# Opening of a two-block network on one core: the first sixteen weight tiles by halves, with GpSimd making half of their low parts

## The chip, the cores and the metric

One core of one Trainium2 chip runs the whole program in one launch. The metric is the device time in microseconds (us) of one execution; the value shown for a kernel is the median of several runs. Engines are named as in the profile: TensorE is PE (its weight loads PEld), VectorE is DVE, ScalarE is ACT, GpSimd is POOL, and the queue that issues most loads is that of SyncE (SP).

## What is computed

Two blocks of layers follow each other on 256 tokens of width 1024, all in float32. The opening of the first is what matters here: a normalised and modulated input is multiplied by an input projection.

```python
def hybrid_layer(x, c, cos, sin, pre_g, post_g, w_ada, b_ada, w_in, w_out):
    B, S, _ = x.shape
    mod = jnp.einsum('bd,de->be', jax.nn.silu(c), w_ada) + b_ada
    shift, scale, gate = jnp.split(mod, 3, axis=-1)
    h = rms_norm(x, pre_g) * (1 + scale[:, None, :]) + shift[:, None, :]
    proj = jnp.einsum('bsd,de->bse', h, w_in)
    qa, ka, va, ga, qb, kb, vb, gb = jnp.split(proj, SPLIT_POINTS, axis=-1)
...
    y = jnp.einsum('bse,ed->bsd', jnp.concatenate([o_a, o_b], axis=-1), w_out)
    y = rms_norm(y, post_g)
    return x + gate[:, None, :] * y
```

`w_ada` is 1024 x 3072 and `w_in` 1024 x 4096. Two such layers (with attention in the part left out) are followed by feed-forward layers, a mixer and a spatial gating unit, which the change does not touch.

## The kernel before

**Products.** A weight tile is 256 rows by 512 columns, held as 128 partitions x 2 x 512 (512 KB); the whole program streams 428 of them. A float32 product is made of three products of rounded parts: ScalarE copies the tile into a buffer `sb_hi` as its high part (type fp32r), VectorE subtracts that from the tile and leaves the low part in the tile's own place (`sb_w..r`). The rows are turned so that the 1024 inputs lie on partitions, in eight chunks of 128 inputs x 256 tokens; they too have a high and a low part (`sb_hT`). TensorE multiplies high by high ("h"), low rows by high weights ("a") and high rows by low weights ("l"), for two groups of 128 tokens and two chunks: twelve matmuls of 128x512 a tile.

**Modulation.** `shift` and `scale` of the first layer come from sixteen tiles of `w_ada` (512 KB each, `sb_w<-in_mw`), two for each chunk of rows. VectorE multiplies such a tile by the condition vector and sums along it in one custom instruction (`dve_vector`, `CUSTOM_DVE_ANT_0 sb_w<-sb_w,sb_rows`), and adds the bias and multiplies the gain in two tiny instructions (`dve_first_end`). The rows of a chunk can be made only after that.

**Order of the opening.** Nothing is scheduled at run time: each engine runs its instructions in the order in which the program writes them (`pe_block1`, `act_block1`, `dve_block1`, `pool_start`, `sp_program`), with waits on semaphores. Before, the first four tiles (two chunks of rows for q, k, v and another q) go through `pe_first_tiles`, which multiplies the first two tiles chunk by chunk, and tiles 4 to 15 go through `pe_unit` one whole tile at a time. TensorE turns all the rows first (`pe_norm`, sixteen transposes). `act_block1` copies the turned rows out of PSUM (`raw`), makes the rows of two chunks at a time (`act_turned`, `act_high`) and the high part of one whole tile at a time (`act_tick`). `dve_block1` mixes whole low parts (`dve_tick`), modulation vectors (`dve_vector`) and the rows' low parts (`dve_low`). GpSimd makes a reciprocal root and fourteen tiny instructions for the angles of the rotary tables (`pool_rope_tables`), then loads the attention mask `blk`. SyncE's queue (`stream_order`) sends two modulation tiles and the first weight tile, two more modulation tiles, three weight tiles, four modulation tiles, and then weight and modulation tiles in turn. `place_stream` gives every load a slot from `release_time`; a load into a slot that is in use waits for its release, and everything behind it in the queue waits with it.

**Behind the opening.** Tiles 16 and up follow, with the attention of the first heads in between: the transposes of q and k (`tq`, `tk`), and the first scores (`("A", 0)`) after tile 15.

## Time and profile before

| | |
|---|---|
| median of 3 runs | 1588.73 us (1588.63 to 1588.76) |
| the profiled execution's own time, first to last instruction (span) | 1587.4 us |
| TensorE busy | 1565.0 us, 99% |
| VectorE busy | 1173.0 us, 74% |
| ScalarE busy | 777.5 us, 49% |
| GpSimd busy | 70.5 us, 4% |
| DMA over the span | 336.97 MB, 212 GB/s on average |

The profile is of one execution. No time is given for it but its span, which is 1.3 us under the median of the runs; sums are made against the span and carried over to the median. A busy TensorE is not TensorE at its peak, since its matmuls overlap. In the timeline a row is one or several like instructions in a run, with start, duration, engine, line, operation, tiles and count, and in square brackets the idle time of the engine just before it and what ended it. Durations of instructions that follow each other overlap a little: a 128x1024 subtraction of VectorE is listed with 1.22 us, and the next starts 1.14 us behind its start.

### The profile page before, as it was taken

The numbers are of one execution on the slowest core, as the hardware profiler recorded it, in microseconds if no ns is written. First come the engines' busy times: TensorE is split into PE (matmuls) and PEld (weight loads), VectorE is DVE, ScalarE is ACT, GpSimd is POOL, SyncE is SP. The second block draws the span as 40 slices with busy tenths as digits, with TensorE's granted clock in tenths as the row PEclk, the third lists the DMA queues.
The fourth block names the chain that finished last, engine by engine and source line by source line (L and its number), as shares of the span: only waits on it lengthen the run. The fifth ranks groups of instructions, "written<-read, shape, count | busy, mean of one in ns | idle before, by whom it ended". The sixth has DMA issues, their size and how long they took to land.

```text
span 1587.4 us, 20744 instructions
## 1 busy us (share of the span) xinstructions
PE 1565.0 (99%) x7994; PEld 1296.9 (82%) x7994; DVE 1173.0 (74%) x1917; ACT 777.5 (49%) x1246; POOL 70.5 (4%) x112
## 2 busy tenths in 40 slices
PE   7999999999999999999999999999999999999998
PEld 5887778888888888887777888888888888888887
DVE  7889899759886665477766888868877667666654
ACT  5767666532222222254556555445555463455552
POOL 2000000100000000030010100000000100010000
PEclk9999999999999999999999999999999999999999
DMA  9977676336656655252122777867777575455550
GB/s 376 373 290 273 234 251 224 107 127 231 213 212 239 224 212 179 87 175 80 67 95 72 281 302 292 311 219 264 255 280 274 210 308 187 171 203 187 186 190 30
DMA packets 93044, 336.97 MB, mean 212 GB/s; under 512 B 10625, under 2 KB 11265, under 8 KB 92690
## 3 DMA queue, kind: packets, MB, share of 16 engines
q1 hardware_dynamic: 90706, 327.58, 57.0%
q0 software_dynamic: 2240, 8.06, 1.5%
q8 instruction: 63, 1.03, 0.3%
q14 instruction: 35, 0.29, 0.1%
HBM read 334.56 MB, written 1.05 MB: 211 GB/s over the span
## 4 chain that ended last, share of the span: by engine, by line
PE 55%; DVE 2%; ACT 1%; issue 0%; POOL 0%; POOLq 0%; DVEq 0%; ACTq 0%
PE bank L292 53%; PE bank L295 2%; DVE sb_tm L301 0%; ACT sb_XN L298 0%; DVE sb_X L301 0%; ACT sb_arena L298 0%; ACT sb_XC L298 0%; DVE sb_arena L319 0%; DVE sb_arena L312 0%; DVE sb_XN L301 0%; DVE sb_sg L316 0%; DVE sb_XC L301 0%; DVE sb_w7r L301 0%; POOL sb_rstd L301 0%; DVE sb_w5r L301 0%
## 5 line engine op out<-in xcount | busy, mean ns | idle before, releaser
L292 PE MATMUL bank<-sb_hT,sb_hi 128*128 128x512 f32 (+1 forms) x1856 | 574.7, 379 | 0.0
L298 ACT ACTIVATE sb_hi<-sb_w 128x1024 fp32r<-128x1024 f32 x428 | 431.1, 1052 | 281.3 <-DMA sb_w<-in_w 238.1
L292 PEld LDWEIGHTS bank<-sb_hT,sb_hi 128*128 128x128 f32 x1856 | 332.1, 188 | 58.5 <-issue 0.2
L292 PE MATMUL bank<-sb_hi,sb_hT 128*128 128x512 f32 x1152 | 369.7, 395 | 2.9 <-ACT sb_hT L298 1.3
L292 PEld LDWEIGHTS bank<-sb_hi,sb_hT 128*128 128x128 f32 x1152 | 215.6, 188 | 53.2 <-issue 5.3
L312 DVE CUSTOM_DVE_ANT_0 sb_w<-sb_w,sb_cb 128x1024 f32<-128x1024 f32 x144 | 175.0, 1220 | 0.0
L301 DVE TENSOR_TENSOR sb_sg<-bank,sb_sg 128x512 f32<-128x512 f32 (+1 forms) x90 | 58.9, 660 | 101.5 <-ACT sb_sg L298 79.7
L298 ACT ACTIVATE sb_sg<-bank 128x512 f32<-128x512 f32 (+1 forms) x98 | 54.8, 573 | 118.0 <-PE bank L292 117.7
L298 ACT ACTIVATE sb_arena<-bank 128x512 f32<-128x512 f32 (+1 forms) x106 | 56.3, 558 | 55.9 <-PE bank L292 32.4
L301 DVE TENSOR_TENSOR sb_tm<-bank,sb_rows 128x512 f32<-128x512 f32 (+1 forms) x41 | 28.1, 684 | 69.5 <-PE bank L292 66.6
L298 ACT ACTIVATE sb_XN<-sb_X 128x512 f32<-128x512 f32 x33 | 20.7, 629 | 99.4 <-DVE sb_X L301 91.5
L301 POOL TENSOR_TENSOR sb_rstd<-sb_rstd,sb_minus_half 128x1 f32<-128x1 f32 (+1 forms) x23 | 14.1, 614 | 1159.0 <-DVE sb_rstd L309 1159.0
L301 DVE TENSOR_TENSOR sb_w1r<-sb_w,sb_hi 128x1024 fp32r<-128x1024 f32 x42 | 51.1, 1217 | 15.4 <-ACT sb_hi L298 15.3
L312 DVE CUSTOM_DVE_ANT_0 sb_w<-sb_w,sb_rows 128x1024 f32<-128x1024 f32 x48 | 57.9, 1221 | 0.8 <-DMA sb_w<-in_mw 0.8
L301 DVE TENSOR_TENSOR sb_w3r<-sb_w,sb_hi 128x1024 fp32r<-128x1024 f32 x42 | 51.4, 1224 | 9.4 <-ACT sb_hi L298 9.3
L301 DVE TENSOR_TENSOR sb_w2r<-sb_w,sb_hi 128x1024 fp32r<-128x1024 f32 x41 | 49.9, 1218 | 7.5 <-ACT sb_hi L298 7.3
L301 DVE TENSOR_TENSOR sb_w0r<-sb_w,sb_hi 128x1024 fp32r<-128x1024 f32 x40 | 48.7, 1218 | 9.0 <-ACT sb_hi L298 9.0
L301 DVE TENSOR_TENSOR sb_w5r<-sb_w,sb_hi 128x1024 fp32r<-128x1024 f32 x36 | 43.9, 1220 | 10.7 <-ACT sb_hi L298 10.7
L312 DVE CUSTOM_DVE_ANT_0 sb_tmw<-sb_w,sb_cb 128x1024 f32<-128x1024 f32 x40 | 48.8, 1220 | 0.9 <-DVE sb_XN L301 0.5
L292 PE MATMUL bank<-sb_hT,sb_w0r 128*128 128x256 f32 (+1 forms) x152 | 47.7, 326 | 0.0
L301 DVE TENSOR_TENSOR sb_w4r<-sb_w,sb_hi 128x1024 fp32r<-128x1024 f32 x32 | 39.0, 1217 | 9.5 <-ACT sb_hi L298 9.5
L301 DVE TENSOR_TENSOR sb_w6r<-sb_w,sb_hi 128x1024 fp32r<-128x1024 f32 x34 | 42.0, 1234 | 5.1 <-ACT sb_hi L298 5.1
(483 smaller groups left out, 3211.4 us busy)
## 6 DMA issues: line engine op xcount, KB each, us to landing
sb_w<-in_w SPq DMA_DIRECT2D x428, 512.0 KB, 4.3
sb_w<-in_mw SPq DMA_DIRECT2D x192, 512.0 KB, 4.8
sb_rows<-in_na_rpb POOLq DMA_DIRECT2D x16, 96.0 KB, 2.9
sb_X<-in_x SPq DMA_DIRECT2D x1, 1024.0 KB, 4.9
sb_cb<-in_cvec POOLq DMA_DIRECT2D x2, 512.0 KB, 8.8
sb_XC<-in_ctx POOLq DMA_DIRECT2D x1, 1024.0 KB, 12.8
sb_arena<-in_sg_ln_g POOLq DMA_DIRECT2D x1, 1024.0 KB, 7.2
sb_arena<-in_sg_ln_b POOLq DMA_DIRECT2D x1, 1024.0 KB, 10.5
```

The source lines that it names most:

```text
L292: return self.e.matmul(out, a, b, start=start, stop=stop)
L295: return self.e.transpose(out, a, ident)
L298: return self.e.activation(out, a, f, **kw)
L301: return self.e.tensor_tensor(out, a, b, op)
L312: return self.e.tensor_tensor_reduce(out=out, in0=a, in1=b, scale=scale, scalar=init, op0=op0, op1=op1, accum_out=accum)
```

## The change

The first sixteen weight tiles are cut into halves, one for each chunk of 128 rows. The work goes in eight steps, one for each chunk of the rows: steps 0 to 5 have four half tiles, step 6 three and step 7 five (`FIRST_UNITS`, `FIRST_STEPS`). SyncE's queue sends a step's two modulation tiles and then its half tiles. In each step VectorE makes the low parts of tiles 0 and 1 of the four and the two modulation vectors for the next step; GpSimd makes the low rows and the low parts of tiles 2 and 3. ScalarE makes the high rows straight from the turned rows, the half tiles' high parts, and the rows' values for GpSimd's subtraction. TensorE takes a step's four halves with all "h" terms first, then "a", then "l". The mask's load stays behind these instructions in GpSimd's program, and the instructions for the angles are spread between them.

```diff
+FIRST_UNITS = [(4 * c2 + i, k) for c2 in range(3) for k in range(2) for i in range(4)]
+FIRST_UNITS += [(12, 0), (13, 0), (14, 0), (12, 1), (13, 1), (15, 0), (14, 1), (15, 1)]
+FIRST_STEPS = [FIRST_UNITS[4 * i:4 * i + 4] for i in range(6)] + [FIRST_UNITS[24:27], FIRST_UNITS[27:]]
...
-    out = [("m", 0), ("m", 1), ("w", 0), ("m", 2), ("m", 3), ("w", 1), ("w", 2), ("w", 3)]
-    out += [("m", n) for n in range(4, 8)]
-    for n in range(4, 16):
-        out += [("w", n)] + [("m", n + 4)] * (n < 12)
+    out = []
+    for step in range(8):
+        out += [("m", 2 * step), ("m", 2 * step + 1)]
+        out += [("w", n, k) for n, k in FIRST_STEPS[step]]
...
+        def act_half_high(e, n, k):
+
+            e.wait_ge(*half_landed(n, k))
+            if HPREV[n] >= 0:
+                e.wait_ge(*done(USED, HPREV[n]))
+            e.act(HI_[HB[n]][:, k, :], ring[SLOT["w", n]][:, k, :], ACT.Copy).then_inc(
+                HI.sem, HI.put(n, *(() if k else (0,))))
...
+        def pool_half_low(e, n, k):
+            s = SLOT["w", n]
+            e.wait_ge(*high_ready(n, k))
+            e.tt(ring_r[s][:, k, :], ring[s][:, k, :], HI_[HB[n]][:, k, :].bitcast(F32), ALU.subtract).then_inc(
+                PO.sem, PO.put("low", n, k))
...
+        def act_first_high(e, ch):
+            t, h, _ = first_rows(ch)
+            e.wait_ge(*modulated("a0sc", ch))
+            e.wait_ge(*done(AE, "raw", ch // 2))
+            e.act(h, t, ACT.Identity, scale=mods[:, TG["a0sc"], ch:ch + 1], bias=mods[:, TG["a0sh"], ch:ch + 1]).then_inc(
+                AE.sem, AE.put("hh", "a0", ch))
...
+        def pool_first_low(e, ch):
+            t, h, l = first_rows(ch)
+            e.wait_ge(*done(AE, "t", "a0", ch))
+            e.tt(l, t, h.bitcast(F32), ALU.subtract).then_inc(PO.sem, PO.put("hl", "a0", ch))
...
+            for step in range(1, 6):
+                for term in "hal":
+                    for i in range(4):
+                        pe_first(e, step // 2 * 4 + i, step % 2, term)
+            for n, k in FIRST_UNITS[24:]:
+                pe_first(e, n, k, "hal")
+                if k or n == 15:
+                    items({(12, 1): 12, (15, 0): 13, (14, 1): 14, (15, 1): 15}.get((n, k)))
...
+                for step in range(1, 8):
+                    units = [u for u in FIRST_STEPS[step] if u != (0, 1)]
+                    if step == 6:
+                        act_rope_tables(e)
+                    act_first_high(e, step)
+                    act_half_high(e, *units[0])
+                    act_first_value(e, step)
+                    for n, k in units[1:]:
+                        act_half_high(e, n, k)
...
+                for step in range(8):
+                    for n, k in FIRST_STEPS[step]:
+                        if n % 4 < 2:
+                            dve_half_low(e, n, k)
+                    if step < 7:
+                        dve_vector(e, 2 * step + 2)
+                        dve_vector(e, 2 * step + 3)
...
+            for step in range(8):
+                if step:
+                    pool_first_low(e, step)
+                for n, k in FIRST_STEPS[step]:
+                    if n % 4 >= 2:
+                        pool_half_low(e, n, k)
+                for _ in range(3):
+                    next(rope, None)
```

How instructions move, first on VectorE, in the middle of the opening. Before, two whole low parts and two vectors stand there (`sb_w..r` is a low part, `sb_w` with `sb_rows` a vector, the line with 128x2 the end of a chunk pair's modulation):

```order
L301 TENSOR_TENSOR sb_w0r<-sb_w_49,sb_hi_78 128x1024
L312 ISA sb_w_51,sb_mods<-sb_w_51,sb_rows_81 128x1024
L312 ISA sb_mods 128x1
L301 TENSOR_TENSOR sb_mods<-sb_mods,sb_vec 128x2x2
L301 TENSOR_TENSOR sb_mods<-sb_mods,sb_vec 128x2
L301 TENSOR_TENSOR sb_w3r<-sb_w_55,sb_hi_71 128x1024
L312 ISA sb_w_57,sb_mods<-sb_w_57,sb_rows_81 128x1024
L312 ISA sb_mods 128x1
L301 TENSOR_TENSOR sb_hT<-sb_sg_84,sb_hT 128x512
```

Now, at a like place (step 3 of the change), each low part is half as long, the pair of them stands together, and the two vectors follow:

```order
L309 TENSOR_TENSOR sb_w10r<-sb_w_118,sb_hi_75 128x512
L309 TENSOR_TENSOR sb_w11r<-sb_w_120,sb_hi_76 128x512
L320 ISA sb_w_130,sb_mods<-sb_w_130,sb_rows_81 128x1024
L320 ISA sb_mods 128x1
L320 ISA sb_w_132,sb_mods<-sb_w_132,sb_rows_81 128x1024
L320 ISA sb_mods 128x1
L309 TENSOR_TENSOR sb_mods<-sb_mods,sb_vec 128x2
L309 TENSOR_TENSOR sb_mods<-sb_mods,sb_vec 128x1
```

Behind this place VectorE has two half low parts for every two vectors, where it had two whole ones and the rows' low part; the second half low part stands ahead of both vectors.

GpSimd, whose program before has only these tiny instructions between the reciprocal root and the mask's load (its end is shown):

```order
L301 TENSOR_TENSOR sb_ang<-sb_kk_100,sb_ang 128x32
L305 TENSOR_SCALAR sb_kk_100<-sb_kk 128x32
L301 TENSOR_TENSOR sb_ang<-sb_kk_100,sb_ang 128x32
L305 TENSOR_SCALAR sb_ang<-sb_ang 128x16
L306 TENSOR_SCALAR sb_ang<-sb_ang 128x32
L331 DMA sb_arena<-in_blk 128x768
```

Now, in steps 4 and 5 (`sb_hT` is the low rows of a chunk):

```order
L309 TENSOR_TENSOR sb_hT<-sb_sg_84,sb_hT 128x256
L309 TENSOR_TENSOR sb_w6r<-sb_w_61,sb_hi_73 128x512
L309 TENSOR_TENSOR sb_w7r<-sb_w_63,sb_hi_74 128x512
L309 TENSOR_TENSOR sb_hT<-sb_sg_84,sb_hT 128x256
L309 TENSOR_TENSOR sb_w6r<-sb_w_61,sb_hi_73 128x512
L309 TENSOR_TENSOR sb_w7r<-sb_w_63,sb_hi_74 128x512
```

Three subtractions a step have come in, the rows' first, and they stand ahead of the mask's load.

ScalarE in step 4 of the change, with high rows, half tiles and the rows' value in one order:

```order
L306 ACTIVATE sb_hT<-sb_sg_84,sb_mods 128x256
L306 ACTIVATE sb_hi_71<-sb_w_49 128x512
L306 ACTIVATE sb_sg_84<-sb_sg_84,sb_mods 128x256
L306 ACTIVATE sb_hi_72<-sb_w_51 128x512
L306 ACTIVATE sb_hi_73<-sb_w_61 128x512
L306 ACTIVATE sb_hi_74<-sb_w_63 128x512
L306 ACTIVATE sb_hT<-sb_sg_84,sb_mods 128x256
```

The high rows of the next chunk are the last of these rows; they stand behind the fourth half tile, and the next step's half tiles stand behind them.

## Rows read from the trace of the kernel before

**Rows 1.** The page, busy time and share of each engine.
```profile
PE 1565.0 (99%) x7994; PEld 1296.9 (82%) x7994; DVE 1173.0 (74%) x1917; ACT 777.5 (49%) x1246; POOL 70.5 (4%) x112
```

**Rows 2.** Timeline of PE in the opening: start and duration in us, count, idle before.
```profile
9.39 3.94 PE L295 MATMUL bank<-sb_cst,sb_XN 128*128 128x128 f32 x16 [3.27 <-ACT sb_XN L298]
...
13.02 1.23 PE L292 MATMUL bank<-sb_hi,sb_hT 128*128 128x512 f32 x4
...
16.13 1.20 PE L292 MATMUL bank<-sb_hi,sb_hT 128*128 128x512 f32 x4 [1.22 <-ACT sb_hi L298]
...
21.48 1.07 PE L292 MATMUL bank<-sb_hi,sb_hT 128*128 128x512 f32 x4
...
24.20 1.07 PE L292 MATMUL bank<-sb_hi,sb_hT 128*128 128x512 f32 x4
...
28.41 0.47 PE L292 MATMUL bank<-sb_hi,sb_hT 128*128 128x512 f32 x1 [1.32 <-ACT sb_hT L298]
...
59.38 1.04 PE L295 MATMUL bank<-sb_cst,sb_arena 128*128 128x128 f32 x8
60.17 0.48 PE L292 MATMUL bank<-sb_hi,sb_hT 128*128 128x512 f32 x1
...
63.07 0.93 PE L292 MATMUL bank<-sb_arena 64*128 64x128 f32 x8
```

**Rows 3.** Window of PE: length, busy (count), granted clock, DMA share, GB/s.
```profile
28.40:61.00 32.60, 32.59 (x152) 1.00 1.03 409
```

**Rows 4.** The page, busy tenths of PE in forty slices of the span.
```profile
PE   7999999999999999999999999999999999999998
```

**Rows 5.** Timeline of DVE, then of POOL, where both work, 285 to 300 us.
```profile
285.36 1.22 DVE L301 TENSOR_TENSOR sb_w7r<-sb_w,sb_hi 128x1024 fp32r<-128x1024 f32 x1
287.10 1.72 DVE L301 TENSOR_TENSOR sb_w6r<-sb_w,sb_hi 128x1024 fp32r<-128x1024 f32 x1 [0.52 <-ACT sb_hi L298]
297.77 1.48 DVE L301 TENSOR_TENSOR sb_w3r<-sb_w,sb_hi 128x1024 fp32r<-128x1024 f32 x1 [1.65 <-ACT sb_hi L298]
286.19 1.54 POOL L301 TENSOR_TENSOR sb_hT<-sb_sg,sb_hT 128x512 fp32r<-128x512 f32 x1 [72.19 <-ACT sb_hT L298]
296.87 1.30 POOL L301 TENSOR_TENSOR sb_hT<-sb_sg,sb_hT 128x512 fp32r<-128x512 f32 x1 [9.13 <-ACT sb_hT L298]
```

**Rows 6.** The same in the opening: DVE, then POOL.
```profile
14.05 1.22 DVE L312 CUSTOM_DVE_ANT_0 sb_w<-sb_w,sb_rows 128x1024 f32<-128x1024 f32 x1
15.20 1.26 DVE L312 CUSTOM_DVE_ANT_0 sb_w<-sb_w,sb_rows 128x1024 f32<-128x1024 f32 x1
14.37 1.01 POOL L301 TENSOR_TENSOR sb_ang<-sb_kk,sb_ang 128x32 f32<-128x32 f32 x1
16.69 0.26 POOL L301 TENSOR_TENSOR sb_ang<-sb_kk,sb_ang 128x32 f32<-128x32 f32 x1
```

**Rows 7.** Timeline of DVE: the modulation and rows of the first chunk.
```profile
11.16 0.36 DVE L301 TENSOR_TENSOR sb_mods<-sb_mods,sb_vec 128x2 f32<-128x2 f32 x2
11.62 0.54 DVE L306 TENSOR_SCALAR sb_sg<-bank,sb_mods 128x256 f32<-128x256 f32 x1
```

**Rows 8.** Timeline of DVE, then of ACT: a vector, additions, rows, a half-size subtraction.
```profile
24.79 1.22 DVE L312 CUSTOM_DVE_ANT_0 sb_w<-sb_w,sb_rows 128x1024 f32<-128x1024 f32 x1
25.94 0.08 DVE L312 DVE_READ_ACCUMULATOR2_ANT sb_mods<- 128x1 f32 x1
28.61 0.69 DVE L301 TENSOR_TENSOR sb_hT<-sb_sg,sb_hT 128x512 fp32r<-128x512 f32 x1
26.51 1.09 ACT L298 ACTIVATE sb_sg<-sb_sg,sb_mods 128x256 f32<-128x256 f32 x2 [1.00 <-DVE sb_mods L301]
27.63 0.63 ACT L298 ACTIVATE sb_hT<-sb_sg 128x512 fp32r<-128x512 f32 x1
```

**Rows 9.** Timeline of DVE, then of POOL, near 1402 us.
```profile
1402.25 1.30 DVE L301 TENSOR_TENSOR sb_hT<-sb_sg,sb_hT 128x256 fp32r<-128x256 f32 x2
1402.40 0.87 POOL L301 TENSOR_TENSOR sb_hT<-sb_sg,sb_hT 128x256 fp32r<-128x256 f32 x1 [0.26 <-ACT sb_hT L298]
```

More of the change, by code:

```diff
@@ L467, in build @@
         slot_load = [signal(f"slot{i}") for i in range(NSLOT + NARENA + NCTX + NXC)]
+        second_load = [signal(f"second{n}") for n in range(16)]
         for i in range(NARENA):
@@ L740, in act_turned @@
             e.wait_ge(*done(TRP, "norm", s, p, c2))
-            if s == "a0" and c2:
-                e.wait_ge(*done(AE, "raw", c2))
             for h in range(2):
@@ L774, in dve_first_chunk, with first_rows, act_raw @@
-        def dve_first_chunk(e):
-            t, h, l = (z[:, 0, :] for z in turned_rows("a0", 0, 0))
-            e.wait_ge(*done(TRP, "norm", "a0", 0, 0))
-            e.wait_ge(*modulated("a0sh", 0))
+        def first_rows(ch):
+            c = slice(ch % 2 * 256, ch % 2 * 256 + 256)
+            return SG[ch // 2][:, c], hTh[:, 0, ch, :], hTl[:, 0, ch, :]
+        def act_raw(e, c2):
+            c = slice(0 if c2 else 256, 512)
+            e.wait_ge(*done(TRP, "norm", "a0", 0, c2))
+            if c2 == 0:
+                e.wait_ge(*done(DE, "chunk", "t"))
+            e.act(SG[c2][:, c], BANK["norm", "a0", 0, c2].ap[:, c], ACT.Copy).then_inc(AE.sem, AE.put("raw", c2))
@@ L781, in dve_first_chunk @@
-            e.wait_ge(DE, DE.n)
-            e.cp(h, t).then_inc(DE.sem, DE.put("chunk", "h"))
+            for o, what in ((h, "h"), (t, "t")):
+                e.ts(o, b, mods[:, TG["a0sc"], 0:1], mods[:, TG["a0sh"], 0:1], ALU.mult, ALU.add).then_inc(
+                    DE.sem, DE.put("chunk", what))
             e.wait_ge(DE, DE.n)
@@ L836, in h_ready @@
             if s == "a0":
-                return done(AE, "hh", s, p, c2) if part == "h" else done(DE, "hl", s, p, c2)
+                return done(AE, "hh", s, kc) if part == "h" else done(PO, "hl", s, kc)
             if c2 % 2 == 0:
@@ L847, in all_split @@
             return [f for s in stages for p in parts_of(s)
-                    for f in (done(DE, "hl", s, p, 2), done(DE if s == "a0" else PO, "hl", s, p, 3))]
+                    for f in ((done(DE, "chunk", "l"), done(PO, "hl", s, 7)) if s == "a0" else
+                              (done(DE, "hl", s, p, 2), done(PO, "hl", s, p, 3)))]
         def rows_turned(s):
@@ L991, in b1_banks, with pe_first @@
             return ("o", l, o // 2 % 2), o % 2 * 2, o < 4 and o % 2 == 0, o >= 4 and o % 2 == 1
-        def pe_first_tiles(e):
-            for u in range(4):
-                key = b1_banks(0, u)[0]
-                BANK[key] = [(AB if u < 2 else TB).take() for _ in range(2)]
-            for u, k in ((0, 0), (1, 0), (0, 1), (1, 1), (2, 0), (2, 1), (3, 0), (3, 1)):
-                h, l, banks = HI_[HB[u]], ring_r[SLOT["w", u]], BANK[b1_banks(0, u)[0]]
-                ah, al = HPARTS
-                e.wait_ge(*done(HI, u))
+        def pe_first(e, n, k, terms):
+            key = b1_banks(0, n)[0]
+            h, l, banks = HI_[HB[n]], ring_r[SLOT["w", n]], BANK[key]
+            kc, last = n // 4 * 2 + k, n >= 12 and k == 1
+            for term in terms:
+                if term == "l":
+                    e.wait_ge(*low_ready(n, k))
+                else:
+                    e.wait_ge(*high_ready(n, k))
+                    e.wait_ge(*h_ready("a0", kc, "h" if term == "h" else "l", 0))
@@ L1011, in pe_first_tiles @@
-                e.wait_ge(*done(LO, u))
-                for x in range(2):
-                    m = e.mm(banks[x].ap[:, :], ah(k, x), l[:, k, :], False, False)
-                if k:
-                    m.then_inc(USED.sem, USED.put(u))
+                    m = e.mm(banks[x].ap[:, :], rows, (l if term == "l" else h)[:, k, :], kc == 0 and term == "h",
+                             last and term == "l")
+                    if term == "l" and k == 1 and x == 1:
+                        m.then_inc(USED.sem, USED.put(n))
+                    elif term == "l" and last:
+                        m.then_inc(ACC.sem, ACC.put(*key, 0))
@@ L1044, in items @@
                         pe_norm(e, "cx0", 0, (i,))
-            for u in range(tail):
+            if l == 0:
+                pe_first_tiles(e, items)
+            for u in range(16 if l == 0 else 0, tail):
                 key, at, first, last = b1_banks(l, u)
-                if l == 0 and u < 4:
-                    continue
                 if first:
@@ L1061, in pe_block1 @@
                         pe_up(e, t0 + u, key, BANK[key], 1, 0, 256, at, ready, True, True, True)
-                        pieces = ()
                     else:
-                        pieces = ("hl", "a") if l == 0 and u in (4, 8, 12) else ("hla",)
-                    for terms in pieces:
-                        pe_unit(e, t0 + u, key, parts, at, BANK[key], (0, 1), ready, first, last and "a" in terms,
-                                used="a" in terms, terms=terms)
+                        pe_unit(e, t0 + u, key, parts, at, BANK[key], (0, 1), ready, first, last)
                 if last:
@@ L1595, in pool_start @@
             pool_rstd(e, "a0")
-            pool_rope_tables(e)
+            rope = pool_rope_tables(e)
+            for _ in range(8):
+                next(rope)
+            for step in range(8):
[6 more added lines that the diff above has]
+                    next(rope, None)
             e.wait_ge(*done(USED, 9))
```

161 lines of the change are left out of this document (86 added, 75 removed).

## The prediction, made before the changed kernel ran

> **What bounds the kernel now.** I read the page's shares first: TensorE (PE) is busy for 99% of the span, VectorE (DVE) for 74%, GpSimd (POOL) for 4% [rows 1]. A gain has to be an idle stretch of TensorE that closes, a loss a new one. The timeline of TensorE shows where it idles in the opening [rows 2]: the first weight product starts at 13.02 us, then come waits of 1.22 us for a high part and of 1.32 us for the turned rows (a shorter one lies between). From 28.41 us on it is never idle up to the first scores at 63.07 us; the window view gives 32.59 us busy in 32.60 [rows 3]. In the page's slices TensorE has a 9 in every slice behind the first, so nothing behind the opening can take up a delay [rows 4]: what the opening loses or gains, the end loses or gains. The last line of rows 2 is the mark for the sum: scores begin at 63.07 us.
>
> The pace: twelve matmuls lie between the starts at 21.48 and 24.20 us [rows 2], so one takes 0.227 us, and a step of the new order (four half tiles, 24 matmuls) 5.44 us. The DMA engines move 409 GB/s [rows 3], so the 2.1 MB of a step (two modulation tiles, four halves) take 5.1 us, a little less than TensorE wants.
>
> Then I read what the helpers do to each other, since the change puts three GpSimd instructions into each step beside VectorE. VectorE's subtraction of 285.36 us lasts 1.22 us, to 286.58. GpSimd's, of 128x512, begins at 286.19 and ends at 287.73, 1.15 us after VectorE's end. VectorE's next begins at 287.10, takes 1.72 us where such a one takes 1.22, and ends at 288.82, 1.09 us after GpSimd's end. In a second case GpSimd ends at 298.17 and VectorE's, begun at 297.77, at 299.25, 1.08 us later [rows 5]. In the opening a GpSimd instruction of 32 columns takes 1.01 us under a vector of VectorE, and ends at 15.38, just after it (14.05 plus 1.22), although VectorE's next vector stood ready and began at 15.20; beside no long instruction one takes 0.26 us [rows 6]. So **one of the two engines stands still while the other runs**, both ways, where both read two operands from SBUF; the custom instruction of the modulation vectors counts too, and they take turns.
>
> The Trainium skill has it as a rule (SBUF — State Buffer, section Who interferes with whom): a VectorE instruction with two SBUF inputs contends with a GpSimd instruction that reads SBUF, and one is blocked for the whole of the other. By that rule, the trace agrees.
>
> **The change part by part.**
>
> 1. *Head.* VectorE's two small additions for chunk 0 end at 11.52 us [rows 7]. The vector table's load moves behind the second modulation tile and its own small addition with it, so these stay where they are. VectorE then writes the first high rows directly, 0.54 us [rows 7], without the copy that followed, and eight transposes instead of sixteen stand ahead of the first product: it starts at about 12.2 us, 0.8 us earlier. The other eight (sixteen take 3.6 us up to 13.02 [rows 2]) move behind the first eight products: the same work, moved.
>
> 2. *VectorE's part of a step:* two half low parts, two vectors, two tiny additions. A 128x512 subtraction is busy for 0.69 us, 0.6 from start to start as a full one's 1.22 is 1.14; a vector takes 1.15 us from start to start (24.79 to 25.94) [rows 8]. By itself 2 x 0.6 + 2 x 1.15 + 0.5 = 4.0 us, under 5.44.
>
> 3. *GpSimd's part of a step:* low rows of 128x256 and two half low parts of 128x512. Directly behind a VectorE instruction these take 0.60 (1402.67, where VectorE's first of two ends by its usual 0.42, to 1403.27 [rows 9]) and 1.15 us, the larger alone 1.30 [rows 5]. That is some 3 us, also under 5.44. Taken in turns with VectorE's 4.0 us it is 7 us, over it.
>
> 4. *The loop of a step.* ScalarE (ACT) works in order, and each of its steps opens with the high rows, which wait for this chunk's modulation; that waits for VectorE's vectors, queued behind VectorE's two half low parts; and the second of these waits for ScalarE. Round the loop, with turns: end of the last vector to ScalarE's start 0.57 us (25.94 to 26.51 [rows 8]); high rows 0.54 and first half of the weights 0.63 (half of the 1.09 for two, and the 128x512 copy [rows 8]); low part 0.61; GpSimd's low rows 0.60, ready by then; second low part 0.56; GpSimd's first half 1.15; vector 1.09; GpSimd's second half 1.15; vector 1.09. The sum is 7.99 us, **8.0 us a step** against TensorE's 5.44. The bounds of the turns: nothing (5.8 us a step, below), and 1.30 us for each GpSimd half, 8.3 us. I take the middle ones because they are measured where the two engines meet.
>
> 5. *The sum.* Rows of chunk 0 are done at 13.1 us (0.54, 0.5 and 0.42 behind 11.6). Then low part 0.6, GpSimd 1.15, low part 0.55, vector 1.15, GpSimd 1.15, vector 1.1, additions 0.57: chunk 1's modulation at 19.4 us. Step 1 has one of its halves made beforehand: 7.3 us, chunk 2 at 26.7. Steps 2 to 5, 4 x 8.0: chunk 6 at 58.7. Step 6 has one GpSimd half fewer, 6.9: chunk 7 at 65.6. Then high rows, a half of the weights and the first product 1.5, GpSimd's low rows another 1.1, and 28 matmuls (6.35) and two groups of eight transposes (0.79 each, 59.38 to 60.17 [rows 2]): 76.1 us. The scores now have one half tile (1.36 us) and not a whole one between the transposes of k and themselves, while ScalarE makes two copies for v and two for k: about 0.3 us of waiting. So 76.4 against 63.07, **plus 13.3 us**.
>
> 6. *Edits at nothing.* The opening's loads, 18.2 MB with x and the tables, take 44 us at 409 GB/s and are in before 50 us, some 20 us before the last is used; the sixteen more DMA issues and pieces of 2 KB per row instead of 4 lie under that lead. Without the turns the lead shrinks to a few us, and the price of the pieces, for which no row stands, would show. GpSimd's load of the mask now stands behind its last half low part, at about 73 us, three us ahead of the scores; should it land late, it holds VectorE, and TensorE only if that lasts longer than the tiles in between (0 to 2 us, I take 0). The sine tables wait for GpSimd's angles, done by 27 us and used in step 6.
>
> The profiled span is 1587.4 us, the runs' median 1588.73; the 1.3 us around the span stay. 1588.73 + 13.3 = 1602.
>
> **The rivals.**
>
> *No turns.* If those overlaps had another cause, each engine would need only its own time. The durations of rows 5, 6 and 9 speak against it. The loop then is 0.57 + 0.54 + 0.56 + 0.55 + 0.63 (high rows, half, value, half on ScalarE) + 0.06 + 0.61 + 2 x 1.15 = 5.8 us, still over 5.44. Chunk 1 at 17.0, chunk 2 at 22.0 (its second modulation tile lands at about 20), five times 5.8: 51.0 for chunk 7, and 10.5 for the tail as above: 61.5 us, 1.5 us early: 1587.3, within 0.2%. The Trainium skill (Advanced Engine Details and Errata, section Mode Summary) names only GpSimd and VectorE's two-port instructions as blocking each other; by that, a subtraction of two tensors at single rate would not collide, and the time would be this rival's.
>
> *Faster.* TensorE is fed without a gap. With products from 12.2 us and low parts in time, step 1 would end at 24.4; before, the same 48 products were through at 26.9 and the next began at 28.41. From there nothing waits: 4.0 us less, 0.3 back at the scores: 1585.0. It decides at a loop of under 5.44 us: no turns, and 0.4 us less in the handovers than the rows show.
>
> *Half of it.* GpSimd stands still for VectorE but not the other way, or turns cost less than in the rows: 1589 to 1597.
>
> *Slower still.* TensorE would idle for a third of the time in the opening. The window shows a granted clock of 1.00 [rows 3]; yet the sixteen transposes at 9.39 us take 0.227 us each and those at 59.38 us 0.10 [rows 2]. If the lower level (1.2 GHz) were granted during the opening, 24 matmuls would take 10.9 us and not 8.0, over seven steps some 20 us more: 1622.
>
> **How the numbers follow.** Turns, my forecast: 0.76, by itself 1598 to 1606 (0.5 us either way on each of five steps, 1 us at the head and the tail). Half of it: 0.06. No turns: 0.09. Faster: 0.05. Slower still: 0.04. The range for 8 in 10 takes in my case and most of the half case: 1592 to 1607. About 0.2%, 3.2 us, is what a measurement of this kernel can tell from no change. Faster by more: 0.05. Within: 0.10 (no turns, and the low end of the half case). Slower by more: 0.85.
>
> **What would show it.** In the profile after: first product near 12.2 us; scores near 76 us; TensorE in the opening some 70% busy, with two waits a step, about 1.7 us for the rows or the first half's high part and 0.7 us for the next half. VectorE's vectors in the opening at 2.2 to 2.3 us instead of 1.22, GpSimd's 128x512 subtractions at 1.3 to 2.4 us. From the scores on the same pattern as before, 13 us later. The forecast is wrong if VectorE's vectors stay at 1.22 us while GpSimd works, or if TensorE is over 90% busy from 28 us on.

## The result and the profile after the change

| | before | after |
|---|---|---|
| median of the runs | 1588.74 us (1588.63 to 1588.97, 4 runs) | 1604.12 us (1603.70 to 1604.23, 4 runs) |
| span of the profiled execution | 1587.4 us | 1602.3 us |
| TensorE busy | 1565.0 us | 1572.7 us |
| first scores | 63.07 us | 77.47 us |

The changed kernel takes 1.0096 times as long (95% interval 1.0084 to 1.0108), 15.4 us more. The forecast was 1602.0, with 1592 to 1607.

The page after, busy time of each engine and busy tenths of TensorE ([rows 1, 4] before):

```profile
PE 1572.7 (98%) x7994; PEld 1298.1 (81%) x7994; DVE 1179.4 (74%) x1919; ACT 779.6 (49%) x1266; POOL 100.5 (6%) x135
...
PE   7899999999999999999999999999999999999998
```

GpSimd has 30 us more work, the largest difference of the page. The same 7994 matmuls show 7.7 us more busy time; the rest of the 14.9 us by which the span grew, 7.2 us, is TensorE idle. Both parts lie ahead of the scores, as the marks of the timeline show. TensorE in the changed kernel (start, duration, count, idle before), to set beside [rows 2]:

```profile
10.25 2.27 PE L303 MATMUL bank<-sb_cst,sb_XN 128*128 128x128 f32 x8 [4.26 <-ACT sb_XN L306]
12.51 3.78 PE L300 MATMUL bank<-sb_hi,sb_hT 128*128 128x512 f32 x8
...
36.58 5.07 PE L300 MATMUL bank<-sb_hi,sb_hT 128*128 128x512 f32 x14 [0.28 <-ACT sb_hi L306]
...
43.43 0.73 PE L300 MATMUL bank<-sb_hi,sb_hT 128*128 128x512 f32 x2
44.44 3.60 PE L300 MATMUL bank<-sb_hi,sb_hT 128*128 128x512 f32 x14 [0.28 <-ACT sb_hi L306]
...
51.31 0.73 PE L300 MATMUL bank<-sb_hi,sb_hT 128*128 128x512 f32 x2 [1.45 <-ACT sb_hi L306]
...
67.29 0.72 PE L300 MATMUL bank<-sb_hi,sb_hT 128*128 128x512 f32 x2 [0.58 <-POOL sb_hT L309]
...
72.67 1.06 PE L303 MATMUL bank<-sb_cst,sb_arena 128*128 128x128 f32 x8 [1.45 <-DVE sb_arena L309]
...
77.47 0.93 PE L300 MATMUL bank<-sb_arena 64*128 64x128 f32 x8
```

A step lasts from 43.43 to 51.31, **7.88 us** for 24 matmuls that need 5.44. The steps that begin at 35.57 and 51.31 us have the same two waits, of about 1.45 us ahead of the first product and 0.28 us behind the second; the one at 43.43 lacks the first, since TensorE was slower in the step before it (its clock, below). The length of the step is the same. The windows of the changed kernel (length, busy time of PE, PEld, DVE, ACT and POOL, then granted clock, DMA share, GB/s), where before had 32.59 of 32.60 us busy at 409 GB/s [rows 3]:

```profile
28.00:61.00 33.00, 26.94 (x100) 18.45 (x99) 26.37 (x35) 14.30 (x31) 18.47 (x14) 0.94 0.93 357
61.00:77.00 16.00, 13.97 (x61) 10.66 (x60) 11.60 (x18) 11.28 (x21) 8.32 (x9) 0.90 0.60 201
77.00:130.00 53.00, 52.89 (x357) 43.68 (x357) 45.30 (x109) 38.32 (x91) 0.00 (x0) 1.00 0.77 284
```

TensorE has gaps up to the scores and hardly any behind (52.89 us busy in 53.00). From the scores to the end both kernels take the same to 0.5 us (1524.8 and 1524.3). One step on the three helpers, first VectorE, then GpSimd, then ScalarE:

```profile
43.41 0.69 DVE L309 TENSOR_TENSOR sb_w0r<-sb_w,sb_hi 128x512 fp32r<-128x512 f32 x1 [1.19 <-ACT sb_hi L306]
44.42 0.82 DVE L309 TENSOR_TENSOR sb_w1r<-sb_w,sb_hi 128x512 fp32r<-128x512 f32 x1 [0.32 <-ACT sb_hi L306]
45.17 2.31 DVE L320 CUSTOM_DVE_ANT_0 sb_w<-sb_w,sb_rows 128x1024 f32<-128x1024 f32 x1
...
47.41 2.30 DVE L320 CUSTOM_DVE_ANT_0 sb_w<-sb_w,sb_rows 128x1024 f32<-128x1024 f32 x1
...
49.75 0.36 DVE L309 TENSOR_TENSOR sb_mods<-sb_mods,sb_vec 128x2 f32<-128x2 f32 x2
```

```profile
43.95 0.75 POOL L309 TENSOR_TENSOR sb_hT<-sb_sg,sb_hT 128x256 fp32r<-128x256 f32 x1 [3.21 <-ACT sb_sg L306]
44.99 1.40 POOL L309 TENSOR_TENSOR sb_w6r<-sb_w,sb_hi 128x512 fp32r<-128x512 f32 x1 [0.29 <-ACT sb_hi L306]
46.35 2.27 POOL L309 TENSOR_TENSOR sb_w7r<-sb_w,sb_hi 128x512 fp32r<-128x512 f32 x1
```

```profile
42.26 0.60 ACT L306 ACTIVATE sb_hT<-sb_sg,sb_mods 128x256 fp32r<-128x256 f32 x1 [4.68 <-DVE sb_mods L309]
...
50.14 0.60 ACT L306 ACTIVATE sb_hT<-sb_sg,sb_mods 128x256 fp32r<-128x256 f32 x1 [4.70 <-DVE sb_mods L309]
```

Read the ends: VectorE's low part ends at 45.24, GpSimd's at 46.39 (1.15 later), VectorE's vector at 47.48 (1.09), GpSimd's second at 48.62 (1.14), VectorE's second vector at 49.71 (1.09). Each engine's duration holds the other's turn: a vector of 1.22 us [rows 8] is listed with 2.30. ScalarE stands 4.7 of the 7.88 us for the modulation, which stands for those two vectors.

### The profile page after: what moved, and what is told of

Read it like the earlier page. It is cut to its first block, busy times and chain, and to the rows that moved or that the text cites. A ratio compares the mean times of both kernels' runs of the same rounds, so it can differ in the third digit from the quotient of the medians.

```text
span 1602.3 us, 20810 instructions
## 1 busy us (share of the span) xinstructions
PE 1572.7 (98%) x7994; PEld 1298.1 (81%) x7994; DVE 1179.4 (74%) x1919; ACT 779.6 (49%) x1266; POOL 100.5 (6%) x135
## 3 DMA queue, kind: packets, MB, share of 16 engines
q8 instruction: 63, 1.03, 0.3%
## 4 chain that ended last, share of the span: by engine, by line
PE 54%; DVE 2%; issue 1%; ACT 1%; POOL 0%; POOLq 0%; DVEq 0%; ACTq 0%
PE bank L300 52%; PE bank L303 2%; DVE sb_tm L309 0%; ACT sb_XN L306 0%; DVE sb_X L309 0%; ACT sb_arena L306 0%; ACT sb_XC L306 0%; DVE sb_arena L327 0%; DVE sb_XN L309 0%; DVE sb_sg L324 0%; DVE sb_arena L320 0%; DVE sb_XC L309 0%; DVE sb_w7r L309 0%; DVE sb_w5r L309 0%; POOL sb_rstd L309 0%
## 5 line engine op out<-in xcount | busy, mean ns | idle before, releaser
L306 ACT ACTIVATE sb_hi<-sb_w 128x1024 fp32r<-128x1024 f32 (+1 forms) x444 | 433.5, 1021 | 270.1 <-DMA sb_w<-in_w 227.3
L306 ACT ACTIVATE sb_sg<-bank 128x512 f32<-128x512 f32 (+2 forms) x99 | 55.1, 571 | 121.2 <-PE bank L300 118.3
L306 ACT ACTIVATE sb_XN<-sb_X 128x512 f32<-128x512 f32 x33 | 20.7, 629 | 99.9 <-DVE sb_X L309 91.0
L320 DVE CUSTOM_DVE_ANT_0 sb_w<-sb_w,sb_rows 128x1024 f32<-128x1024 f32 x48 | 68.8, 1455 | 0.3 <-ACT sb_rows L306 0.3
L309 DVE TENSOR_TENSOR sb_w2r<-sb_w,sb_hi 128x1024 fp32r<-128x1024 f32 (+1 forms) x43 | 51.5, 1198 | 17.0 <-ACT sb_hi L306 17.0
L309 DVE TENSOR_TENSOR sb_w3r<-sb_w,sb_hi 128x1024 fp32r<-128x1024 f32 (+1 forms) x45 | 53.8, 1195 | 10.1 <-ACT sb_hi L306 10.0
L309 DVE TENSOR_TENSOR sb_w0r<-sb_w,sb_hi 128x1024 fp32r<-128x1024 f32 (+1 forms) x40 | 47.6, 1190 | 10.8 <-ACT sb_hi L306 10.8
L309 DVE TENSOR_TENSOR sb_w1r<-sb_w,sb_hi 128x1024 fp32r<-128x1024 f32 (+1 forms) x41 | 49.1, 1197 | 7.3 <-ACT sb_hi L306 7.3
L309 DVE TENSOR_TENSOR sb_w5r<-sb_w,sb_hi 128x1024 fp32r<-128x1024 f32 (+1 forms) x36 | 43.0, 1194 | 11.5 <-ACT sb_hi L306 11.5
L309 DVE TENSOR_TENSOR sb_w4r<-sb_w,sb_hi 128x1024 fp32r<-128x1024 f32 (+1 forms) x35 | 41.6, 1189 | 13.0 <-ACT sb_hi L306 13.0
L320 DVE CUSTOM_DVE_ANT_0 sb_tmw<-sb_w,sb_cb 128x1024 f32<-128x1024 f32 x40 | 48.7, 1218 | 0.6
L309 POOL TENSOR_TENSOR sb_hT<-sb_sg,sb_hT 128x256 fp32r<-128x256 f32 (+1 forms) x39 | 33.7, 864 | 172.0 <-ACT sb_hT L306 153.8
```

The lines of the kernel that those rows point to most:

```text
L306: return self.e.activation(out, a, f, **kw)
L309: return self.e.tensor_tensor(out, a, b, op)
L320: return self.e.tensor_tensor_reduce(out=out, in0=a, in1=b, scale=scale, scalar=init, op0=op0, op1=op1, accum_out=accum)
```

## The experiments

Eleven more kernels ran. Theory A ("turns"): VectorE and GpSimd block one another, and the loop of a step (modulation, high rows, high part, two low parts, two vectors) is stretched by GpSimd's turns. Rival B: GpSimd's subtractions are merely slow, and TensorE waits for them. Rival C: the head of the opening (the order of transposes, loads and chunk 1) sets the loss.

### 1. GpSimd writes without reading

```diff
-            e.tt(ring_r[s][:, k, :], ring[s][:, k, :], HI_[HB[n]][:, k, :].bitcast(F32), ALU.subtract)...
+            e.memset(ring_r[s][:, k, :].bitcast(F32), 0.0)...
+            e.wait_ge(PO, PO.n)
+            e.memset(ring_r[s][:, k, :].bitcast(F32), 0.0)...
```

> The changed kernel, but GpSimd sets the low parts of its sixteen half tiles to zero (two fills each, no read) where it subtracted; its rows' low parts stay as they are. The low parts of these tiles are thereby left out of the product. Turns (GpSimd's reading stops VectorE): a fill reads nothing, so VectorE's vectors go back from 2.30 to about 1.2 us and a step from 7.88 to about 5.9 us; time about 1593 us. Rival, GpSimd is merely slow and its results come late: the fills take about as long as the subtractions, so the step stays at 7.9 us and the time at 1604 us.

Measured: 1591.24 us against 1588.89 (ratio 1.0013, 1.0003 to 1.0023), scores at 64.57. VectorE, then GpSimd:

```profile
38.45 1.21 DVE L320 CUSTOM_DVE_ANT_0 sb_w<-sb_w,sb_rows 128x1024 f32<-128x1024 f32 x1
...
39.60 1.21 DVE L320 CUSTOM_DVE_ANT_0 sb_w<-sb_w,sb_rows 128x1024 f32<-128x1024 f32 x1
```

```profile
38.24 1.11 POOL L336 MEMSET sb_w6r<- 128x512 f32 x2 [0.27 <-ACT sb_hi L306]
39.30 1.11 POOL L336 MEMSET sb_w7r<- 128x512 f32 x2
```

GpSimd is at work for 2.2 us under the two vectors and they take 1.21 us each. VectorE's step, from first low part to first low part, takes 5.71 us; TensorE, which still has a lead on it, takes 5.44 to 5.51 us a step up to 48.7 us. It is not GpSimd's activity, its writes or its semaphores that cost VectorE time: 12.9 of the 15.4 us go with the reads of its half low parts. Two fills stand for one subtraction and last nearly as long as its turn (1.06 us against 1.15), so the time that GpSimd needs for a half tile is hardly less (1.11 us listed, against 1.29 for an undisturbed subtraction): B would have expected a step close to 7.9 us.

### 2. Half low parts on VectorE

```diff
-            return done(PO, "low", n, k) if n % 4 >= 2 else done(LO, n) if k else done(LO, n, 0)
+            return done(LO, n) if k else done(LO, n, 0)
...
                     for n, k in FIRST_STEPS[step]:
-                        if n % 4 < 2:
-                            dve_half_low(e, n, k)
+                        dve_half_low(e, n, k)
```

> The changed kernel with all weight low parts on VectorE; GpSimd keeps only the low rows (one instruction of 128x256 a step). Turns: the step is 0.57 + 1.1 + 4 x 0.61 + 0.6 for the rows' turn + 2 x 1.15, about 7.0 us with the loop through ScalarE still closed, against 7.88; time about 1598 us. Rival, halves alone (pieces, order of products) are the cost: no change from 1604 us. Rival, nothing but GpSimd is the cost: step 5.8 us or less and 1590 us or less.

Measured: 1599.39 us (ratio 1.0065, 1.005 to 1.008), a step of 6.90 us against the 7.0 of the first theory, scores at 72.65. VectorE takes over two subtractions of 0.60 us a step, and the step gets 0.98 us shorter: two turns of GpSimd cost 2.2 us, two turns of VectorE's own 1.2. GpSimd's help has a negative worth here. But 6.90 is still far above 5.44, so turns are not the whole of it; the order is the other part.

### 3 and 4. The vectors ahead of the low parts

Run 3 has from step 1 on the vectors for the next chunk ahead of this step's low parts, so that the modulation no longer waits for ScalarE's high parts. Run 4 does that and makes all low parts, the rows' too, on VectorE.

```diff
-                    for n, k in FIRST_STEPS[step]:
-                        if n % 4 < 2:
-                            dve_half_low(e, n, k)
-                    if step < 7:
-                        dve_vector(e, 2 * step + 2)
-                        dve_vector(e, 2 * step + 3)
+                    for part in ("lv" if step == 0 else "vl"):
...
```

> The changed kernel, but from step 1 on VectorE makes the next step's two modulation vectors before this step's half low parts, so that the next modulation no longer waits for ScalarE's halves. GpSimd's work is unchanged. Turns: the two engines' times still add up, 4.0 + 2.9 = 6.9 us a step, time about 1598 us. Rival, the loop through ScalarE is the cost and turns are not: TensorE's own 5.4 us a step and 1587 us or less.

> Vectors first as in the run before it, and every low part (weights and rows) on VectorE; GpSimd has only the angles. Turns: VectorE alone needs 4 x 0.61 + 0.36 + 2 x 1.15 + 0.45, about 5.6 us a step, just over TensorE's 5.44, no turns after the angles; scores near 59 us and time about 1586 us, under the kernel before. Rival, the halves themselves (small pieces in the queue, more instructions) cost: 1590 us or more.

Run 3: 1596.74 us (ratio 1.005, 1.0035 to 1.0065), step 6.42 us, scores at 69.11. Run 4: 1590.44 us (1.0011, 1.0001 to 1.0021), step 5.42 us, scores at 63.64. Moving two vectors takes 7.4 us off the changed kernel with GpSimd's turns still there (the four runs of run 3 spread over 2.5 us, so this is known to about 1 us). The step is shorter than the 6.9 us of the first theory, and longer than TensorE's own 5.4 us of its rival. Run 2's edit alone takes off 4.7 us, run 3's 7.4, and run 4, which has both and the rows' low parts too, 13.7 of the 15.4: turns and order each hold a part of the loop. In run 3 the turns fall on VectorE's other instructions instead, its tiny additions too:

```profile
40.35 1.76 DVE L320 CUSTOM_DVE_ANT_0 sb_w<-sb_w,sb_rows 128x1024 f32<-128x1024 f32 x1
...
42.15 2.36 DVE L309 TENSOR_TENSOR sb_mods<-sb_mods,sb_vec 128x2 f32<-128x2 f32 x2
44.43 0.68 DVE L309 TENSOR_TENSOR sb_w0r<-sb_w,sb_hi 128x512 fp32r<-128x512 f32 x1
```

Run 4 has VectorE busy without a pause, 5.42 us a step against TensorE's 5.44. I had expected 1586 us of it and scores at 59; the 1590.44 us are what the rival of that run had set down for small pieces and more instructions. Most of the miss is ahead of the steady steps: they begin at 27.63 us, where 48 matmuls and eight transposes without a wait from 12.34 us on would have ended at about 24.0 (0.227 and 0.10 us each). Another 0.88 us is a wait for the low rows of chunk 6 (below). In the head VectorE stood 2.27 us for a high part, behind a copy of turned rows on ScalarE:

```profile
17.31 0.69 DVE L309 TENSOR_TENSOR sb_w5r<-sb_w,sb_hi 128x512 fp32r<-128x512 f32 x1 [2.27 <-ACT sb_hi L306]
```

```profile
16.16 0.60 ACT L306 ACTIVATE sb_sg<-bank 128x512 f32<-128x512 f32 x1 [2.41 <-PE bank L303]
```

### 5, 6 and 9. What holds the head

Run 5 is run 4 with all sixteen transposes ahead of the first product, run 6 also loads the positions behind the first weight tile, run 9 also loads chunk 2's modulation tiles two half tiles earlier.

```diff
-            pe_norm(e, "a0", 0, (0, 1))
+            pe_norm(e, "a0", 0, (0, 1, 2, 3))
...
-            pe_norm(e, "a0", 0, (2, 3))
...
-            e.dma(posi[:, :], I["positions"][:, :])...
+                if n == 6:
+                    e.dma(posi[:, :], I["positions"][:, :])...
...
+        out += halves[:2] + [("m", 4), ("m", 5)] * (step == 1) + halves[2:]
```

> Run e4 with all sixteen transposes ahead of the first product, as before the change. In e4 VectorE stood 2.27 us for a high part that ScalarE makes behind the copy of bank 2, and that copy waited for the second eight transposes. If that chain is what e4 loses at the head: the wait goes, chunk 1's modulation at about 18.7 us instead of 20.7, step still 5.4 us, scores at about 61.7, time 1588.5 us. If something else sets the head (VectorE's own work there, or the landing of the tiles): no change, 1590.4 us.

> Run e5 with the load of the positions moved from ahead of x to behind the first modulation and weight tiles. The normalised rows came 0.8 us later than in the kernel before in every run with the positions ahead. If that load held x back: first transposes at 9.4 us again, everything 0.7 us earlier, 1587.8 us, and a little under the kernel before (1588.9). If the late start has another cause: as e5.

> Run e6 with the two modulation tiles of chunk 2 loaded behind the second half tile of step 1 and no longer behind the fourth. In e6 VectorE stood 1.57 us at 17.6 us for the first of them to land, and from there on ran its 5.42 us a step without a pause, with TensorE waiting for it three times. If that landing is what still holds the head: the wait shrinks below 0.5 us, chunk 2's modulation at 20.6 us instead of 21.9, scores at 62.3 instead of 63.4, time 1588.7 us, level with or a little under the kernel before. If the two half tiles that now land later (2.6 us) hold TensorE in step 1 as long: 1589.8 us again.

Measured: run 5 1590.25 us (ratio 1.001, 1.0 to 1.0019), run 6 1589.84 (ratio 1.0007, 0.9998 to 1.0016), run 9 1589.91 (1.0008, 0.9999 to 1.0016). The scores begin at 63.67, 63.44 and 63.85 us. The times hoped for were 1588.5, 1587.8 and 1588.7 us: all three missed. Each edit changed what stood at its place, and almost nothing came of it. In run 5 the wait of 2.27 us is gone and chunk 1's modulation is there at 18.3 us instead of 20.7. In run 6 the transposes begin at 9.43 us again and not at 9.94, as x lands at 6.05 us and not at 6.56. In the seven kernels with the positions' load ahead of x it lands at 6.49 to 6.86 us, in five of the six with it behind at 6.00 to 6.16; but in run 9, where it is behind too, at 6.50. So the load most likely holds x back by about 0.5 us, and something else can as well. But now VectorE waits for loads, in run 6:

```profile
19.15 1.23 DVE L320 CUSTOM_DVE_ANT_0 sb_w<-sb_w,sb_rows 128x1024 f32<-128x1024 f32 x1 [1.57 <-DMA sb_w<-in_mw]
...
36.15 1.23 DVE L320 CUSTOM_DVE_ANT_0 sb_w<-sb_w,sb_rows 128x1024 f32<-128x1024 f32 x1 [0.48 <-DMA sb_w<-in_mw]
```

The profiled execution of run 9 is the slowest of its eleven (1590.57 us), so its rows are compared with care. VectorE takes the first of these tiles at 18.07 us without a wait, chunk 2's modulation is done at 21.1 us instead of 22.1, and later pairs wait in its place, VectorE in run 9:

```profile
24.69 1.23 DVE L322 CUSTOM_DVE_ANT_0 sb_w<-sb_w,sb_rows 128x1024 f32<-128x1024 f32 x1 [0.79 <-DMA sb_w<-in_mw]
...
36.65 1.23 DVE L322 CUSTOM_DVE_ANT_0 sb_w<-sb_w,sb_rows 128x1024 f32<-128x1024 f32 x1 [0.88 <-DMA sb_w<-in_mw]
```

Four heads that lie up to 2.3 us apart when VectorE begins chunk 1's low rows (23.28, 22.48, 22.00 and 21.00 us) meet again four steps later: it begins chunk 5's low rows at 44.98 us in run 4, 45.02 in run 5, 44.78 in run 6 and 45.19 in run 9. In runs 5, 6 and 9 the lead is given back in waits for loads; run 4 comes to the same time without one, at its own 5.42 us a step. Two limits lie close together here, VectorE's own work and the landing of the modulation tiles. The kernel before, then run 6, window of 28 to 38 us, columns as above:

```profile
28.00:38.00 10.00, 9.59 (x42) 7.98 (x43) 9.93 (x16) 5.70 (x8) 0.00 (x0) 1.00 1.03 407
```

```profile
28.00:38.00 10.00, 10.00 (x45) 8.26 (x45) 9.32 (x18) 5.90 (x12) 0.00 (x0) 1.00 1.04 395
```

The DMA engines are as busy in both and move 12 GB/s (3%) less where weight tiles come in halves; from 50 to 56 us, where whole tiles come again, run 6 has 410 GB/s. So the smaller pieces look like the reason, for which the prediction had no row. Over the 31 us from 19 to 50 us such a rate makes about 0.9 us. Run 6 lacks 1.1 us against before, but that the two are the same is not shown, and the rows speak for more than one cause: its scores come only 0.37 us later, the times behind the scores differ by another 0.3, and the last wait of TensorE ahead of the rotary code is one for low rows, which is there in run 4 too, where VectorE waited for no load. TensorE in run 4, then in run 6:

```profile
50.88 0.73 PE L300 MATMUL bank<-sb_hi,sb_hT 128*128 128x512 f32 x2 [0.88 <-DVE sb_hT L309]
```

```profile
50.68 0.73 PE L300 MATMUL bank<-sb_hi,sb_hT 128*128 128x512 f32 x2 [1.04 <-DVE sb_hT L309]
```

From step 6 on the products go half tile by half tile (all three terms of one, then the next), so the low rows are wanted behind two matmuls and no longer behind eight. No run beat the kernel before; the intervals of runs 5, 6 and 9 reach down to no difference.

### 7 and 11. The disputed cost alone

The kernel before, unchanged but for twelve subtractions of GpSimd on memory that nobody uses then and for which nobody waits: a tile of 512 columns less itself (run 7), two different tiles of 448 columns (run 11).

```diff
+            spare = XC[:, 1, 512:1024]
+            e.memset(spare, 0.0)...
+            for i in range(12):
+                e.wait_ge(PO, PO.n)
+                e.tt(spare, spare, spare, ALU.subtract)...
```

> The kernel before, with twelve GpSimd subtractions of 128x512 on spare memory behind the angles, from 20.4 us on, which nobody waits for (ahead of GpSimd's later loads). By turns: each vector and full low part of VectorE that meets one takes 2.3 us instead of 1.22, GpSimd's 1.3 to 2.5 us, VectorE falls back by about 12 x 1.15 = 13.8 us less what lead it has (2 to 4 us), scores 8 to 12 us later, 1597 to 1601 us. If GpSimd's subtractions are merely slow and VectorE is not touched: vectors 1.22 us, time within 1 us of before.

> Run e7 with subtractions of two different operands, 448 columns, in place of a tile less itself, 512 columns. In e7 a turn of GpSimd cost VectorE 0.84 us (1.98 us from vector to vector instead of 1.14), where 512 columns cost 1.09 to 1.15 in the rows of before and after. If the same operand twice made it cheaper: 448 columns cost 0.95 to 1.0 us, 2.1 us from vector to vector, time 1599 us. If a turn is dearer only where low parts are written as the matmul's type: 0.73 us, 1.87 us, 1596.7 us.

Measured: run 7 1597.70 us (ratio 1.0057, 1.0043 to 1.0071), scores at 71.50; run 11, one execution, 1599.13. VectorE, then GpSimd in run 7, and VectorE in run 11:

```profile
23.71 2.05 DVE L312 CUSTOM_DVE_ANT_0 sb_w<-sb_w,sb_rows 128x1024 f32<-128x1024 f32 x1
...
25.69 2.05 DVE L312 CUSTOM_DVE_ANT_0 sb_w<-sb_w,sb_rows 128x1024 f32<-128x1024 f32 x1
```

```profile
21.28 21.81 POOL L301 TENSOR_TENSOR sb_XC<-sb_XC 128x512 f32<-128x512 f32 x12
```

```profile
25.10 2.16 DVE L312 CUSTOM_DVE_ANT_0 sb_w<-sb_w,sb_rows 128x1024 f32<-128x1024 f32 x1
...
27.19 2.14 DVE L312 CUSTOM_DVE_ANT_0 sb_w<-sb_w,sb_rows 128x1024 f32<-128x1024 f32 x1
```

Twelve instructions off every chain of data cost 8.9 us. This shows the lock without any of the change's code, and B, by which VectorE is not touched, falls. TensorE's clock fell in run 7 as well, behind a wait of 4.54 us. TensorE in run 7, then a window of it (length, busy, granted clock, DMA share, GB/s):

```profile
30.84 0.77 PE L292 MATMUL bank<-sb_hi,sb_hT 128*128 128x512 f32 x1 [4.54 <-ACT sb_hT L298]
```

```profile
31.00:33.00 2.00, 2.00 (x5) 0.50 1.03 412
```

It is not what the end pays for: behind it TensorE waits 0.94 us for VectorE's low parts twice and 0.67 us for rows, so VectorE, 9.0 us late by then (48.54 us for the low part that stood at 39.54), still sets the time.

The size differs: a turn costs VectorE 0.84 us in run 7 (1.98 from vector to vector, less 1.14) and 0.95 in run 11 for fewer columns, as the first of its two alternatives had it. Subtracting a tile from itself is cheaper here than subtracting two different ones. Run 11 is one execution, so its time is only a rough one; its rows are clear.

### 8. The head of the change alone

The changed kernel with only the transposes and the positions' load moved as in run 6.

> The changed kernel with the two edits of e5 and e6 alone (sixteen transposes first, positions later); turns and order of the steps as in the change. The step stays 7.9 us; chunk 1's modulation 0.7 to 1.5 us earlier than its 19.35, scores at 76.0 to 76.8, time 1602.6 to 1603.4 us: by this, the head is a small part of the loss of 15.4 us and the steps the rest. If the head fed the steps in another way: more than 2 us less.

Measured: 1602.36 us (ratio 1.0085, 1.0072 to 1.0099), scores at 75.40. Chunk 1's modulation is there 2.6 us earlier (16.75 us), and 1.8 us of it reach the end, somewhat more than expected: one later step takes 9.0 us instead of 7.9, with VectorE's two low parts at 1.84 and 1.22 us where they take 0.69 and 0.82, so more turns of GpSimd fall into it. With the turns and the order left as they are, C accounts for 1.8 of 15.4 us.

### 10. GpSimd reads one operand

```diff
-            e.tt(ring_r[s][:, k, :], ring[s][:, k, :], HI_[HB[n]][:, k, :].bitcast(F32), ALU.subtract)...
+            e.cp(ring_r[s][:, k, :], ring[s][:, k, :])...
```

> The changed kernel with GpSimd's sixteen half low parts made by a plain copy of the half tile: one operand read from SBUF, one written; the subtraction of the high part is left out. Fills (run e1, no operand read) let VectorE's vectors run at 1.21 us, subtractions (two read) made them 2.30. If any read of GpSimd's blocks VectorE: vectors at 1.21 plus the copy's time (0.6 to 1.1), step 6.9 to 7.9 us, time 1598 to 1604 us. If only an instruction that reads two operands blocks: vectors 1.21 us, step 5.7 us, 1591 us as in e1.

Measured: 1594.87 us (ratio 1.004, 1.0025 to 1.0055), a step of 6.52 us. VectorE, then GpSimd:

```profile
39.52 1.63 DVE L320 CUSTOM_DVE_ANT_0 sb_w<-sb_w,sb_rows 128x1024 f32<-128x1024 f32 x1
...
41.07 1.62 DVE L320 CUSTOM_DVE_ANT_0 sb_w<-sb_w,sb_rows 128x1024 f32<-128x1024 f32 x1
```

```profile
40.01 1.61 POOL L327 CAST sb_w7r<-sb_w 128x512 fp32r<-128x512 f32 x1
...
59.16 0.61 POOL L327 CAST sb_w14r<-sb_w 128x512 fp32r<-128x512 f32 x1
```

One read operand is enough to block, against the second theory of this run. The price was below the first one's range, and so were the step and the time: 1.55 us from vector to vector, so 0.41 us a turn. For 512 columns a turn costs nothing with no operand read, 0.41 with one and 1.09 with two.

The Trainium skill (GPSIMD Engine Reference, Elementwise — side-by-side cycle accounting) gives GpSimd 1.03 cycles per element for a body bound by its ports and 2.6 for two inputs. An estimate by that page, at 1.2 GHz: 0.44 and 1.11 us for 512 columns and 0.97 for 448; by that rule, the traces agree (0.41, 1.09 and, in run 11, 0.95 us). The tile less itself, with two inputs and 0.84 us in run 7, does not fit it.

## Why the prediction was right, step by step

- **Head, step 1 of the prediction: small misses.** First product 12.51 us, not 12.2. The transposes begin at 10.25 us instead of 9.39, and the additions for chunk 0 end at 11.71 instead of 11.52. The positions' load stands ahead of x now, a queue step I had passed over, and x lands at 6.86 us instead of 6.01; part of that is this load (run 6). The first eight products take 0.45 us each and not 0.227. The head's share of the loss is small (run 8).
- **The turns, steps 2 and 3: right.** Vectors 2.30 us (forecast 2.2 to 2.3), GpSimd's 128x512 1.3 to 2.3 us, turn 1.15 and 1.09. Runs 1, 7, 10 and 11 show the mechanism with no, one and two operands read. In the Trainium skill the two rules of the prediction part here: the one of SBUF — State Buffer (section Who interferes with whom) fits, blocking by a second SBUF input against a GpSimd read, and a GpSimd instruction that only writes going free; that of Advanced Engine Details and Errata (section Mode Summary) names only VectorE's two-port instructions, and by it, as the prediction read it, the rival without turns would have come; it did not.
- **The loop, step 4: right, 7.88 for 7.99 us.** The rows add up link by link to 7.88: end of the second vector (49.71) to ScalarE's start 0.43, 1.15 to the first low part, 1.01 to the second, 0.75 to the first vector, 2.24 and 2.30 for the two. One link had another reason than I gave: the second low part waits for ScalarE's next high part and not for GpSimd's turn; both end at nearly the same time.
- **The sum, step 5: chunks right, tail mis-sized.** Modulation of chunk 1 at 19.35 (forecast 19.4), chunk 2 at 26.5 (26.7), chunk 6 at 58.0 (58.7), chunk 7 at 64.8 (65.6). Then the term "10.5, plus 0.3 of waiting" measured 12.7 us. Up to the product with chunk 7's low rows it held (2.5 us, 2.6 in the sum). From there the 28 matmuls took 7.1 us and not 6.35, and the waiting was 1.45 us, for the rotary rows of q ahead of the transposes, and not 0.3. ScalarE had made the high part of a whole tile ahead of the copy that the rotary code wants, and that code on VectorE ran in turns with GpSimd's last low parts:

```profile
68.50 1.05 ACT L306 ACTIVATE sb_hi<-sb_w 128x1024 fp32r<-128x1024 f32 x1
69.45 1.06 ACT L306 ACTIVATE sb_arena<-bank 128x512 f32<-128x512 f32 x2
```

```profile
70.54 1.53 DVE L309 TENSOR_TENSOR sb_tm<-sb_arena,sb_rcs 128x256 f32<-128x256 f32 x2 [2.76 <-ACT sb_arena L306]
```

  Chunk 7 was 0.8 us early, the tail 1.9 late: scores 14.4 us later instead of 13.3, so that part of the tail's miss is hidden by luck. The median moved by 15.4; the last 1.0 us, 0.5 of it behind the scores and 0.5 outside the profiled execution's difference of spans, I did not trace. The part behind the scores belongs to the change, not to the noise of one profile: from the scores to the end the kernel before and runs 7 and 11 take 1524.2 to 1524.3 us, and all that have the first tiles in halves 1524.5 to 1525.0.
- **Costs taken as nothing, step 6: right for the time.** The mask's load is issued at 71.39 us and no wait of TensorE ends on it. The loads run at 397 GB/s from 19 to 50 us instead of 410, and at 280 from 50 to 61 us, where SyncE's queue waits for slots that VectorE and TensorE free later. That the lead over the loads would be gone without the turns came true in runs 5, 6 and 9, where VectorE waits for them; what of their 1.1 to 1.5 us over the kernel before is the price of the pieces stays open.
- **"TensorE some 70% busy", with waits of 1.7 and 0.7 us: wrong in its parts.** It is 82% busy, and the two waits are 1.45 and 0.28 us. The matmuls behind a wait run slower than 0.227 us each, so what they lack in idle time they show as busy time; the length of the step is that of the loop through VectorE and ScalarE either way.
- **The rival "slower still"**: its condition came true in places and its price did not. The clock fell in two stretches, to 0.69 in 36.5 to 42 us and 0.62 in 60 to 64.5 us. The fourteen matmuls at 36.58 took 5.07 us instead of 3.60, yet that step lasted 7.86 us, as the others: TensorE had 2.4 us to spare. TensorE in the changed kernel, windows as above:

```profile
36.50:42.00 5.50, 5.42 (x17) 4.27 (x18) 5.40 (x6) 1.07 (x3) 3.94 (x3) 0.69 1.04 393
42.00:60.00 18.00, 14.46 (x57) 9.59 (x55) 13.48 (x19) 8.76 (x20) 9.05 (x7) 1.00 0.86 328
60.00:64.50 4.50, 4.00 (x11) 3.15 (x12) 4.28 (x6) 0.67 (x2) 1.83 (x2) 0.62 0.66 267
```

- **The rival "no turns"** forecast 5.8 us a step and no loss; run 1, the nearest to it, has 5.71 us a step and 2.4 us of loss. TensorE's steps are not longer there (5.44 to 5.51 us); its waits are in the head, and behind 48 us (0.17, 0.46, 0.58 and 0.69).
